# The first stage of a two-block transformer kernel: later parameter loads, earlier fourth keys and first key norm

## The reference

```python
# second_block, computed first by the kernel
mem_kv = rms_norm_2(mem, mem_norm) @ mem_wkv            # (256, 1024) @ (1024, 2048)
mem_k, mem_v = jnp.split(mem_kv, 2, axis=-1)
mem_k = rms_norm_2(mem_k.reshape(1, 256, 4, 256), mem_knorm)   # four heads, each normed
...
# first_block
h = layer_norm(x, ln_in_g, ln_in_b)
for l in range(2):
    proj = h @ w_in[l]                                   # (256, 1024) @ (1024, 1888)
    ...                                                  # four branches: conv, attention, gate, latent attention
    h = layer_norm(ALPHA * h + mix @ w_out[l], ...)
    ...                                                  # convolved feed-forward, layer norm
```

## Time and profile before

| | us |
|---|---|
| median of 3 runs | 1793.12 |
| lowest, highest | 1792.72, 1794.09 |
| profiled execution | 1794.38 |
| its span | 1792.6 |

### The profile page before, as it was taken

One profiled execution on the slowest core, in us unless ns is written; L12 is line 12 of the kernel. 1 busy time (PEld: TensorE's weight loads), 2 busy tenths in 40 slices (PEclk: granted clock), 3 DMA queues, 4 the chain that ended last, 5 costly groups with the idle time before them and its releaser, 6 DMA issues.

```text
span 1792.6 us, 28818 instructions
## 1 busy us (share of the span) xinstructions
PE 1761.7 (98%) x10644; PEld 1547.7 (86%) x10657; DVE 1319.7 (74%) x1782; ACT 958.9 (53%) x1293; POOL 98.4 (5%) x90
## 2 busy tenths in 40 slices
PE   8999999999999999999999999999999999999999
PEld 7978998896898988888998988888888886888887
DVE  6999877799987787666787656666666677557666
ACT  5556555547555555445546555444644467655443
POOL 1001100000300000000170000000000000000000
PEclk9999999999999999999999999999999999999999
DMA  9626755553574637555534635555555541525553
GB/s 333 181 99 197 253 190 179 164 157 117 183 263 168 210 124 258 189 185 164 178 110 164 240 114 183 192 187 187 187 192 186 197 142 50 186 95 194 187 197 125
DMA packets 236626, 318.51 MB, mean 178 GB/s; under 512 B 14342, under 2 KB 206758, under 8 KB 236038
## 3 DMA queue, kind: packets, MB, share of 16 engines
q1 hardware_dynamic: 230838, 295.44, 49.6%
q0 software_dynamic: 5424, 20.35, 3.5%
q10 hardware_dynamic: 288, 1.69, 0.2%
HBM read 313.27 MB, written 4.19 MB: 177 GB/s over the span
## 4 chain that ended last, share of the span: by engine, by line
PE 88%; DVE 7%; ACT 2%; issue 2%; DMA 1%; SPq 1%; DVEq 0%; ACTq 0%
PE bank L1070 20%; PE bank L1055 20%; PE bank L744 16%; PE bank L1073 10%; PE bank L946 7%; PE bank L767 2%; DVE w_lo L2402 2%; PE bank L753 1%; PE bank L772 1%; PE bank L831 1%; PE bank L1230 1%; DVE work L2399 1%; ACT w_hi L1738 1%; PE bank L1152 1%; SPq L3603 1%
## 5 line engine op out<-in xcount | busy, mean ns | idle before, releaser
L2402 DVE TENSOR_TENSOR w_lo<-raw,w_hi 128x2048 fp32r<-128x2048 f32 (+2 forms) x283 | 639.6, 2265 | 208.9 <-ACT w_hi L1738 205.9
L1738 ACT ACTIVATE w_hi<-raw 128x2048 fp32r<-128x2048 f32 (+2 forms) x278 | 527.5, 1900 | 292.3 <-PE bank L1070 156.0
L1070 PE MATMUL bank<-xt_both,w_hi 128*128 128x512 f32 x1600 | 400.3, 392 | 0.0
L1070 PEld LDWEIGHTS bank<-xt_both,w_hi 128*128 128x128 f32 x1600 | 291.6, 189 | 54.6
L744 PE MATMUL bank<-xt_both,w_hi 128*128 128x256 f32 (+1 forms) x1840 | 334.7, 284 | 0.2
L744 PEld LDWEIGHTS bank<-xt_both,w_hi 128*128 128x128 f32 (+1 forms) x1840 | 285.3, 190 | 2.5 <-issue 1.6
L1738 ACT ACTIVATE work<-bank 128x256 f32<-128x256 f32 (+3 forms) x290 | 120.8, 427 | 283.3 <-PE bank L1073 256.9
L744 PE MATMUL bank<-xt_both,w_lo 128*128 128x256 f32 (+2 forms) x920 | 260.1, 283 | 0.0
L1073 PEld LDWEIGHTS bank<-xt_both,w_lo 128*128 128x128 f32 x1600 | 218.3, 190 | 15.6
L1073 PE MATMUL bank<-xt_both,w_lo 128*128 128x256 f32 x1600 | 223.1, 282 | 0.0
L1055 PE MATMUL bank<-w_hi,act_hi 128*128 128x512 f32 x528 | 206.7, 392 | 0.2
(11 more groups left out here) (362 smaller groups left out, 1960.8 us busy)
## 6 DMA issues: line engine op xcount, KB each, us to landing
raw<-in_ffn_wi SPq DMA_DIRECT2D x88, 1024.0 KB, 5.1
raw<-in_ffn_w_up SPq DMA_DIRECT2D x44, 1024.0 KB, 5.1
raw<-in_ffn_wo SPq DMA_DIRECT2D x44, 1024.0 KB, 4.9
raw<-in_ffn_w_down SPq DMA_DIRECT2D x22, 1024.0 KB, 5.3
raw<-in_ssd_in_proj SPq DMA_DIRECT2D x14, 1024.0 KB, 5.4
raw<-in_w_in SPq DMA_DIRECT2D x8, 1024.0 KB, 7.1
raw<-in_w_out SPq DMA_DIRECT2D x8, 1024.0 KB, 4.9
raw<-in_even_out_proj SPq DMA_DIRECT2D x8, 1024.0 KB, 4.8
```

The source lines that it names most:

```text
L1070: first(mm(bank[b][:, :], w[0][:, k, P * j:P * j + P], xt_both[:, k, :, :].rearrange("p v t -> p (v t)"), start=k == 0, stop=False))
L1738: return act.activation(dst, src, ACT.Copy)
L2402: return dve.tensor_tensor(out=out, in0=in0, in1=in1, op=op)
```

## The change

Three edits, all in the first stage. ACT empties and squares the fourth keys ahead of its split of in0.0. DVE norms the keys of head 0 one split earlier, ahead of in0.0's low half. SP issues all 38 late parameter loads behind mem5 instead of a quarter behind each of mem2 to mem5; nothing else in its order changes, and the same loads are made.

```diff
@@ -1824,8 +1824,8 @@
                     act.activation(sd[:, tt:tt + 1], mv[:, tt, 1:2], ACT.Sqrt, bias=eps[:, 0:1]).then_inc(sd_ready, 1)
                 deviation("mem", 0)
                 deviation("mem", 1)
-                split()
                 key(3)
+                split()
                 split()
                 b = full("memv4")
                 drained("memv4", copy(mem_v[:, :, 0:256], b[:, :]))
@@ -2585,8 +2585,8 @@
                     if j == 3:
                         for tt in range(TT):
                             center_scale(tt, z[:, tt, :], x[:, tt, :]).then_inc(z_ready, 1)
+                        memory_key(0)
                     if j == 4:
-                        memory_key(0)
                         memory_key(1)
                 dve.wait_ge(turned_sum, 1)
                 take_stream("x0", None, biased=True)
@@ -3590,18 +3590,14 @@
                 sp.wait_ge(stage_clear, 1)
                 for dst, src in stage_loads(True):
                     sp.dma_start(dst, src).then_inc(early_in, 16)
-                late, sent = stage_loads(False), 0
                 for j in range(MEM_UNITS):
                     columns(f"mem{j}", inp["mem_wkv_2"], 256 * j, 256)
                     if j == 3:
                         for tt in range(TT):
                             sp.dma_start(x[:, tt, :], inp["x"][0, P * tt:P * tt + P, :]).then_inc(x_in, 16)
 
-                    if j >= 2:
-                        upto_row = STAGE_DMAS * (j - 1) // 4
-                        for dst, src in late[sent:upto_row]:
-                            sp.dma_start(dst, src).then_inc(stage_in, 16)
-                        sent = upto_row
+                for dst, src in stage_loads(False):
+                    sp.dma_start(dst, src).then_inc(stage_in, 16)
 
             def mixer(l):
                 w = inp["w_in"][l]
```

More of the change, by code:

```diff
@@ L1826, in start @@
                 deviation("mem", 1)
+                key(3)
                 split()
-                key(3)
                 split()
```

## The result

| | before | changed |
|---|---|---|
| median, 20 runs each, us | 1793.03 | 1796.87 |
| lowest, highest | 1791.36, 1795.42 | 1793.95, 1798.73 |
| profiled execution | 1794.38 | 1795.74 |
| its span | 1792.6 | 1793.9 |

The ratio is 1.0019, 95% interval 1.0013 to 1.0026: slower by 3.4 us (2.3 to 4.7); the medians of the table are 3.8 us apart. I had said 1790.0, faster by 3.1. The profiled execution is one of the quicker of the changed kernel, 1.1 us under its median, so it shows less than the whole loss.

What follows compares the result with a forecast made beforehand. PE, 98% busy, bounds the kernel, with holes at L767 and L1006. Earlier mixer 1.93 us (containing 0.97) and clock 1.5 put PE 3.4 ahead; DVE's 3.1 counts: 1793.12 - 3.1 = 1790.0, range 1788.2 to 1793.6.

Steps and rivals of the forecast that it cites:

- key(3) ahead of the split on ACT: ACT, first stage: fourth keys run in idle time to about 41.5, removing PE's 0.97 us wait at L1006.
- memory_key(0) ahead on DVE: DVE, first stage: 2.57 us of key norm fits the pause from 42.2; cast near 52.5, PE gains 1.93 us.
- The parameters on SP: SP behind mem5: 38 issues take 15.3 us plus 1.5 allowed; in0.0 issued at 38.2, landing 43.3; cost 0 to 0.1.
- rival 2: SP: late loads starve the mixer, issues take some 22 us; +4.0, 1797.1; decides from in0.0 issued after 40.2; chance 0.06.
- The slack of 0.5 us: DVE before the stream's cast: 0.5 us of slack against 52.5, so in0.0's low half 0.4 later costs 0 to 0.1.
- The clock: PE behind the hole before the mixer: hole of 1.05 us keeps 2.4 GHz; gain 1.7 less 0.2, bounds 0 and 1.7.
- Rival 4: PE before L1296: being ahead also shortens the 2.1 us hole and its low clock; 1.2 more, 1788.8; chance 0.12.
- What follows: After the stream: PE 3.4 us ahead, DVE catches up in pauses at 77 and 88 to 3.06; 3.1 us counts.

Runs made afterwards that it cites:

- E3: Kernel before with only key(3) moved ahead of in0.0's split on ACT; 1792.74 us, ratio 0.9996 to the kernel before.
- E2: Kernel before with only the two key edits, parameter loads left spread between the memory units; 1789.45 us, ratio 0.9976 to the kernel before.
- E6: Key edits on the kernel before; 19 parameter loads left in place, then mem5 and in0.0 together, then 19; 1790.32 us, ratio 0.9983 to the kernel before.
- E5: Changed kernel with in0.0 issued directly behind mem5, ahead of the 38 parameter loads; 1798.92 us, ratio 1.0026 to the kernel before.
- E12: Changed kernel with 18 matmuls on zeros in PE's long hole ahead of the mixer; 1793.69 us, ratio 0.9998 to the kernel before.
- E1: Kernel before with only the parameter loads moved behind mem5, old order on ACT and DVE; 1797.02 us, ratio 1.0019 to the kernel before.
- E10: Changed kernel with 9 parameter loads left between the memory units and 29 behind mem5; 1791.56 us, ratio 0.9984 to the kernel before.
- E9: Changed kernel with 19 parameter loads left between the memory units and 19 behind mem5; 1790.72 us, ratio 0.9984 to the kernel before.
- E8: Kernel before with 6 matmuls on zeros in PE's 2.0 us hole ahead of the mixer; 1791.80 us, ratio 0.9993 to the kernel before.
- E11: Key edits on the kernel before, plus 8 matmuls on zeros ahead of L1296 in both mixers; 1788.25 us, ratio 0.9967 to the kernel before.

## Why the prediction was wrong, step by step

- **key(3) ahead of the split on ACT: right.** It ran at 39.2 to 40.4 and the wait at L1006 went. That its 0.97 us is contained in the other edit's gain, not added, is what E3 showed.
- **memory_key(0) ahead on DVE: right.** 41.2 to 43.9, in the pause. In E2 the cast came at 52.09, forecast 52.5.
- **The parameters on SP: the step that failed.** "With no stall in0.0 is issued at 36.7; I allow 1.5 us: 38.2" was 42.14: the 38 issues took 19.9 us where I had 15.3 + 1.5 = 16.8, and they began at 22.3 instead of 21.4, since mem5's own issue took 1.3 us instead of 0.4. 3.1 + 0.9 us is the whole error, and the term that was mis-sized is the 1.5 us allowed for stalls: the 38 took 4.6 us more than my 15.3 without stalls, and the first two alone took 3.7 us more than the 0.25 that such a load takes. The terms behind it held: landing 5.4 us after the issue (forecast 5.1), in0.1 3.1 us behind (3), decided beyond an issue at 40.2. I had argued that the stalls belong to x and the constants in flight. In E6 and E5 a parameter stalled for 4.05 us at 26.95 and for 3.39 at 28.17, after x had landed (26.6, 26.3). They go with the place and not with the load: in_ssd_norm took 3.06 us where it stood first behind mem4, and 0.29 in the changed kernel, where it stands further back. The size could have been read from the kernel before, on SP, where the same two loads stood first behind mem2:

```profile
6.21 2.59 SPq L3603 DMA_DIRECT2D work<-in_conv_a_w  x1
8.84 1.46 SPq L3603 DMA_DIRECT2D work<-in_xattn_qnorm  x1
```

They took 2.73 and 1.46 us when they stood first behind mem5. That the rows with stalls summed to some 22 us stood in my own rival 2.
- **The slack of 0.5 us was on the wrong load.** It was worked out for in0.0. What ACT's order makes decisive is in0.1 (E5), and there the slack is nothing: in E2 its split already begins at its landing (45.82).
- **The clock: right with the key edits, and the second half of the loss without them.** E2's hole of 1.25 us left it at 1.00. The hole of 5.1 us in the changed kernel costs 3.8 us by E12's ratio, some part of which may be chance behind the other holes; the profiles show 1.2 us of it ahead of the mixer, and E5's 1.7 us more in the mixer. Rival 4's reason, that the hole before L1296 shrinks, was false: it stayed 2.1 us everywhere.
- **What follows: nearly right.** The key edits gave 4.2 us by medians in E2, where I had 3.1; at L1187 PE was 3.65 us ahead, at L1296 3.6. DVE took nothing back.
- **The balance.** By the ratios: key edits -4.3 (E2, good to 1.8 us), lateness of in0.1 +3.9 (E12 less E2, to some 2.4), clock +3.8 (changed kernel less E12, to some 2.0), together the +3.4 measured. The split depends on the order: from E1 one would put down +3.4 to the loads and nothing to the key edits. Rival 2 named the mechanism, the order of size and the deciding point, with 1797.1 against 1796.87. That the number is so near is partly luck, since the clock's share was not added; 0.06 was far too small a chance for it. Its condition lay 2 us from my central value, in a term for which I allowed 1.5 us although the rows showed more.

What makes an issue stall is open. The long stalls stand at the first loads behind a freshly issued weight load, but not behind each: in the kernel before the first ones behind mem3 and x take 0.35 us and behind mem5 0.65. Those of 0.9 to 1.5 us near 35 to 38 us occur in the changed kernel, E6 and E10 and not in E9, and no run isolates them.

## What to carry to other kernels

Small loads are dear on the queue that issues them, not in bytes: ahead of a weight load in program order, 38 of them were 19.9 us, and at the end of it, from 40 to 45 us, the DMA engines were busy 0.47 of the time. Spread between loads that wait for a slot anyway they cost nothing that these runs show, so a block of them should only be gathered where nothing on the same queue is due. And when one queue holds up an engine's order, fix the order behind it first: two moves of 1.2 and 2.6 us of work gained 4.2 us with the loads in time and nothing measurable with them late. In the fixed order each microsecond of in0.1 then delays the mixer by one.

## What the runs showed of the hardware beyond that

A hole of PE of 2.1 us is a toss-up: the granted clock fell to 1.2 GHz after 14 of 26 of them and held 2.4 GHz after the rest, with nothing else different that I can see. After the eight holes of 1.25 us before the mixer it fell in none of the profiles; it fell after the two of 1.94 and 2.03 us there and after all four holes of 3.5 us and more. Matmuls on zeros kept it up in all four holes profiled with them (E8, twice E11, E12). The prediction took the fall for certain at 2 us, from three falls in three; the spread of single runs, some 4 us for one kernel, has room for these throws. POOL issued the 38 loads in 0.52 us each on average, without a long stall, while SP needed 0.25 to 4.05 us for one; in all both took 19.9 us.
